# Windowed sink attention in a fused transformer kernel: scores in two fp32r products from stacked high and low halves, one key projection, query projections three tiles ahead

## The chip, the cores and the metric

One core of one Trainium2 chip runs the kernel. The metric is device time in microseconds for one execution, lower is better. Matrix products run on TensorE (PE in the rows), elementwise work on VectorE (DVE) and ScalarE (ACT), some sums on GpSimd (POOL), and SyncE (SP) issues the weight stream. DVE, ACT and PE each take their instructions in the order of their program and meet at semaphores.

## What is computed

Two stacked blocks on 512 tokens of width 1024: an HGRN2 mixer and a convolutional FFN, then shared keys and values with a windowed sink attention and a second FFN, then a latent attention (MLA) and a Hyena mixer. The change touches the windowed attention alone:

```python
k, v = split(rms_norm(h, kv_norm) @ w_kv, 2)             # 2 key/value heads of 64
q = (x @ w_q).reshape(nb, 128, 2, 8, 64)                 # 16 query heads of 64
kb, vb = band(k), band(v)                                # the block before and the own block
scores = einsum('nqkgd,nskd->nkgqs', q, kb) * 64 ** -0.5
scores = where(valid, scores - slopes * dist, -inf)      # 0 <= dist < 128, key_abs >= 0
m = maximum(max(scores), sink)
e = exp(scores - m)
probs = e / (sum(e) + exp(sink - m))
out = einsum('nkgqs,nskd->nqkgd', probs, vb) @ w_o
```

There are four blocks of 128 queries, each with 256 keys. The first block has no block before it, so 128 of its 256 keys are always masked.

## The kernel before

Activations lie transposed: channels on partitions, 512 tokens on the free axis. A weight matrix is streamed in chunks of eight 128x128 tiles. Nearly every product is made in three fp32r passes: the fp32 weights `raw` and the activations are split into a high part (rounded to fp32r, on ACT: `whi`, `khi`) and a low part (the rest, on DVE: `wlo`, `klo`), and `mm_w` adds high x high, high x low and low x high. I call these three matmuls on one 128x128 weight tile a *tile*. A projection (`project`) is eight tiles into one PSUM bank.

The stage `swa` has five parts. (1) Projections: query projection 0 (`wq` 0) and 1, two key projections (`kv` 0 and 1) of eight tiles each, where the weights hold each key head twice, so that it comes out on both halves of the partitions. DVE writes them into `kz`, zeroed ahead by POOL: for key head kv and half x the other half stays zero, and one query tile `qb` with two query heads on its two halves can be used whole. (2) `value_rows`: the values, tokens on partitions, 96 matmuls of 128 columns. (3) Eight *pairs* of query heads, 0 to 7. (4) The output projection `wo`, eight times eight tiles. (5) The residual and the next norm.

A pair i goes through these steps. PE makes the scores, 4 blocks x 2 heads, plain fp32, 128 queries x 256 keys (`softmax`, L685). DVE adds the distance bias into `s` (L2276, eight instructions; the first of them I call the *start* of pair i), takes the maxima (L2281) and makes the negated maximum (L2287). ACT exponentiates in eight instructions with row sums (L1488), then takes the exponential of the sink (L1493). DVE adds, inverts and scales the eight rows (L2299). PE transposes them, four per block (L707, `turn`), ACT copies each block to `pt` (L1503), PE multiplies by the values (L726, fp32), and ACT and DVE split the result into `khi` (L1515) and `klo` (L2307).

The three engines run generators woven by hand. In *round* i they work at `softmax(i + 1)`, `values(i)` and the projection of pair i + 2. On PE a round is: scores of i + 1; then by `SWA_TILES` the eight tiles of projection i + 2, two at a time, with the steps of `values(i)` between them. In rounds 6 and 7, where no projection is left, 6 and 8 tiles of the output projection take their place (`begin`). DVE and ACT use `SWA_AHEAD`: what the projection needs of them comes in the first and middle steps, the exponentials in steps 0 to 3, the sink's exponential in step 4.

## Time and profile before

| | |
|---|---|
| time, median of 3 runs | 2037.94 us (2037.1 to 2038.3) |
| span of the profiled execution | 2037.5 us, 24678 instructions |
| PE / DVE / ACT busy | 97% / 68% / 41% of the span |
| the stage's first query scores, start | 760.64 us |
| start of pair 1, of pair 7 | 778.55, 863.12 us |
| last gap of PE in the stage, end | 887.34 us |

The profile is of one execution, and its own time, first to last instruction, is the span of 2037.5 us; no launch time lies around it in this profile. It is 0.4 us under the median of the runs. A row of the timeline has the start in us from the span's start, the duration, the engine, the line and the operation with its tiles, and in brackets the idle time before it with what ended that. Rows that follow one another overlap a little, since an engine begins an instruction while the end of the one before is still being written; so what an instruction costs in a sequence is the distance from start to start, which I call its pitch. An fp32 matmul of the code is two instructions in the trace (16 rows of scores per pair for 8 in the code).

### The profile page before, as it was taken

The page shows a single profiled execution, that of the slowest core. Times are in us where ns is not written, and L with a number is a line of the kernel's source. Part 1 is how long each engine was busy: PE and PEld are TensorE (multiplying, and loading weights), DVE is VectorE, ACT ScalarE, POOL GpSimd, SP SyncE. Part 2 cuts the span into 40 slices and gives each one's busy share as a digit, 9 for nine tenths or more (in the row PEclk, how much of TensorE's full clock was granted, in tenths as well). Part 3 has the DMA queues.
Part 4 walks back from the last instruction along what each step waited for, and adds up shares of the span by engine and source line. Part 5 has one row for each costly group of instructions (what it writes and reads, how often), then busy time and mean ns, then how long its engine had stood idle before and what let it go on. Part 6 is the DMA issues. An engine that isn't in the chain of part 4 may idle for free.

```text
span 2037.5 us, 24678 instructions
## 1 busy us (share of the span) xinstructions
PE 1978.4 (97%) x9878; PEld 1655.8 (81%) x9878; DVE 1380.5 (68%) x1961; ACT 828.0 (41%) x1259; POOL 233.3 (11%) x234
## 2 busy tenths in 40 slices
PE   8999999999999999999999999999999989999997
PEld 6888887788888888888888888778888878888786
DVE  5577765997789667756764784555555567787774
ACT  5233334442233245544432443444344444454442
POOL 2132231003201230010000001000000101000011
PEclk9999999999999999999999999999999989999998
DMA  5211112345534341114344333311111323232421
GB/s 182 72 56 54 61 53 85 130 150 179 201 138 157 132 137 34 40 64 147 137 159 135 126 133 99 108 62 42 42 32 42 114 73 124 93 126 81 145 94 52
DMA packets 60963, 208.40 MB, mean 102 GB/s; under 512 B 6832, under 2 KB 7152, under 8 KB 59696
## 3 DMA queue, kind: packets, MB, share of 16 engines
q1 hardware_dynamic: 53296, 193.19, 27.9%
q10 hardware_dynamic: 7552, 13.64, 1.9%
q8 instruction: 78, 1.28, 0.2%
q14 instruction: 37, 0.30, 0.0%
HBM read 196.31 MB, written 10.49 MB: 101 GB/s over the span
## 4 chain that ended last, share of the span: by engine, by line
PE 79%; DVE 13%; ACT 5%; issue 2%; POOL 1%; DMA 0%; ACTq 0%; DVEq 0%; SPq 0%
PE PS L324 21%; PE PS L328 20%; PE PS L327 20%; DVE wlo L1879 2%; PE PS L436 2%; PE PS L933 2%; PE PS L331 1%; PE PS L335 1%; PE PS L334 1%; ACT whi L1196 1%; PE PS L922 1%; PE PS L685 1%; PE PS L386 1%; PE PS L726 1%; DVE col_f L2094 1%
## 5 line engine op out<-in xcount | busy, mean ns | idle before, releaser
L324 PE MATMUL PS<-nhi,whi 128*128 128x512 f32 x1456 | 593.1, 407 | 15.4 <-DVE wlo L1879 3.7
L328 PE MATMUL PS<-nhi,wlo 128*128 128x512 f32 x1456 | 571.8, 393 | 0.0
L327 PE MATMUL PS<-nlo,whi 128*128 128x512 f32 x1456 | 570.6, 392 | 0.0
L1879 DVE TENSOR_TENSOR wlo<-raw,whi 128x1024 fp32r<-128x1024 f32 x291 | 368.4, 1276 | 176.5 <-ACT whi L1196 175.4
L1196 ACT ACTIVATE whi<-raw 128x1024 fp32r<-128x1024 f32 x291 | 303.3, 1052 | 209.0 <-PE PS L324 133.2
L324 PEld LDWEIGHTS PS<-nhi,whi 128*128 128x128 f32 x1456 | 276.1, 190 | 78.4 <-issue 11.3
L328 PEld LDWEIGHTS PS<-nhi,wlo 128*128 128x128 f32 x1456 | 275.3, 189 | 59.7
L327 PEld LDWEIGHTS PS<-nlo,whi 128*128 128x128 f32 x1456 | 276.4, 190 | 53.5 <-issue 2.6
L2723 POOL TENSOR_TENSOR diag<-diag,sqb 128x512 f32<-128x512 f32 (+1 forms) x56 | 73.6, 1314 | 780.9 <-ACT sqb L1205 698.3
L324 PE MATMUL PS<-hh_f,whi 128*128 128x512 f32 x352 | 137.8, 392 | 0.0
L327 PE MATMUL PS<-hl_f,whi 128*128 128x512 f32 x352 | 137.7, 391 | 0.0
L328 PE MATMUL PS<-hh_f,wlo 128*128 128x512 f32 x352 | 137.5, 391 | 0.0
L2739 POOL TENSOR_TENSOR sd_f<-ab_f 128x512 f32<-128x512 f32 x32 | 55.3, 1745 | 271.7 <-DVE ab_f L2182 271.1
L2094 DVE SCALAR_TENSOR_TENSOR col_f<-aw_f,scv,col_f 128x1024 f32<-128x1024 f32 x63 | 85.0, 1358 | 0.0
L328 PEld LDWEIGHTS PS<-hh_f,wlo 128*128 128x128 f32 x352 | 66.5, 189 | 14.0
L324 PEld LDWEIGHTS PS<-hh_f,whi 128*128 128x128 f32 x352 | 66.4, 189 | 13.9
L327 PEld LDWEIGHTS PS<-hl_f,whi 128*128 128x128 f32 x352 | 66.5, 189 | 13.7
L1419 ACT ACTIVATE t_f<-gp_f,par 128x512 f32<-128x512 f32 x44 | 35.9, 816 | 94.3 <-DVE gp_f L2199 94.3
L1665 ACT ACTIVATE pt_m<-PS 128x768 f32<-128x768 f32 x32 | 25.9, 811 | 111.8 <-PE PS L922 111.8
L1923 DVE TENSOR_TENSOR hT<-hT,PS 128x512 f32<-128x512 f32 x48 | 32.8, 682 | 52.2 <-PE PS L328 52.1
L436 PEld LDWEIGHTS PS<-qa,kk 128*128 128x128 f32 x448 | 56.0, 191 | 14.2 <-DVE qa L2031 10.3
L1205 ACT ACTIVATE sqb<-hT 128x512 f32<-128x512 f32 x42 | 26.3, 629 | 94.7 <-DVE hT L1923 62.5
(356 smaller groups left out, 3373.2 us busy)
## 6 DMA issues: line engine op xcount, KB each, us to landing
raw<-in_stream SPq DMA_DIRECT2D x291, 512.0 KB, 3.5
aw_f<-in_ada SPq DMA_DIRECT2D x48, 512.0 KB, 4.4
rows<-sd_f ACTq DMA_DIRECT2D x32, 256.0 KB, 2.2
rows_h<-rows SPq DMA_DIRECT2D x8, 1024.0 KB, 6.1
wd_f<-in_decay ACTq DMA_DIRECT2D x16, 256.0 KB, 3.0
hT<-in_xT SPq DMA_DIRECT2D x8, 256.0 KB, 6.9
out<-hT SPq DMA_DIRECT2D x8, 256.0 KB, 2.0
wd_f<-in_filt_out ACTq DMA_DIRECT2D x8, 128.0 KB, 2.9
```

Of the source, the lines that this page charges most:

```text
L324: op = e.matmul(out, hi, xh, start=first, stop=False)
L327: e.matmul(out, hi, xl, start=False, stop=False)
L328: return e.matmul(out, lo, xh, start=False, stop=last)
L436: op = e.matmul(B[b][:, cs], kk[:, z, cs], qx[:, cs], start=True, stop=True)
L933: op = e.matmul(B[6][:, 128 * blk:128 * blk + 128], a.v[:, t, 128 * h:128 * h + 128], a.pt[:, i, 128 * t:128 * t + 128], start=t == 0, sto ...
L1196: e.activation(m.whi[:, c % HL, :], m.raw[:, c % RAW, :], ACT.Copy).then_inc(*s.w_hi.tick(c))
L1419: e.activation(a.t[:, 0, z, :], a.gp[:, z, 2:T + 2], ACT.Identity, bias=pc(cb, f), scale=pc(cw, 44 + f)).then_inc(*s.made_a.tick("c0", lay ...
L1879: e.tensor_tensor(m.wlo[:, c % HL, :], m.raw[:, c % RAW, :], m.whi[:, c % HL, :].bitcast(F), SUB).then_inc(*s.w_lo.tick(c))
L1923: op = e.tensor_tensor(h, h, B[b], ADD)
L2094: e.scalar_tensor_tensor(col[:, v, :], aw[:, n % AW[layer], :], m.scv[:, 2, k, v:v + 1], col[:, v, :], MUL, ADD).then_inc(*s.made_v.tick(" ...
L2723: e.tensor_tensor(acc, acc, m.sqb[:, i % 2 if site != "n4" else 0, 0:width], ADD).then_inc(*s.acc.tick(site, i))
L2739: e.tensor_tensor(a.sd[:, x, :], a.ab[:, 0, :], a.ab[:, 1, :], SUB if x else ADD).then_inc(*s.made_p.tick("sd", n, i, x))
```

## The change

The scores are now two fp32r matmuls. The query tile `qt` is split into `qs`: for half x of the partitions, that head's high part stands on its own half and its low part on the other half (128 rows: 64 high, 64 low). The keys are laid out as `kh`, the high part on both halves, and `kl`, the low part on both halves. `qs` times `kh` plus `qs` times `kl` is the whole product (high and low of the query against the high, then against the low part of the key). `kz` and its zeroing are gone, and the mask tile has one form. One key projection is left instead of two, its high and low parts being copied to both halves by ACT and DVE (four instructions each). Block 0 works on its own 128 keys alone in every step. PE has the second query projection after the key projection, takes value tiles ahead of each block's scores of pair 0, runs the query projections three tiles ahead of the rounds, and has 21 rather than 14 tiles of the output projection before the last values end (one more output is begun).

```diff
+++ after.py
@@ -194,12 +194,14 @@
...
+        a.kh, a.kl = p("kh", [128, 2, T], FR), p("kl", [128, 2, T], FR)
         a.vz = p("vz", [128, 4, 2, 2, 128])
...
+        a.qt = p("qt", [128, 2, T])
+        a.qs = p("qs", [128, 2, 2, T], FR)
         a.s = p("s", [128, 2, 8, 256])
         a.pt = p("pt", [128, 4, 512])
-        a.dist = p("dist", [128, 2, 256])
+        a.kt = a.pt[:, 0, :]
+        a.dist = p("dist", [128, 256])
         a.sm = p("sm", [128, 2, 8, 8])
     with ExitStack() as cs:
         call = m.call = sbt(cs, "call", [128, 2 * KD * TC], FR)
@@ -276,8 +278,12 @@
...
 HG_TILES = [0, 0, 3, 2, 2, 2, 2, 2, 2, 2, 1, 1, 1, 3, 0, 1]
-SWA_TILES = [2, 2, 2, 2, 1, 1, 1, 1, 1]
+SWA_LEAD = 3
+SWA_TILES = [2, 2, 1, 0, 0, 1, 1, 1, 0]
 SWA_AHEAD = [7, 0, 0, 1, 1, 1, 1, 1, 1]
+SWA_BEGUN = [0] * 6 + [1] * 7 + [0] + [2] * 7
+SWA_LAST = {KD - 2: 11, KD - 1: 10}
+head_keys = lambda blk: slice(128, 256) if blk == 0 else slice(0, 256)
...
-        run(project(5, "wq", 1, ("wq", 1), nhi, nlo, lambda: q.wait_ge(*s.h.at("down0", 1, 5)),
-                    then={5: spread("n2")}))
 
         def ready(k):
             q.wait_ge(*s.hid_lo.at("kv", k))
 
-        for n in range(2):
-            run(project(n, "kv", n, ("kv", n), khi, klo, lambda: q.wait_ge(*s.h.at("down0", 1, 6 + n)), ready))
+        run(project(0, "kv", 0, ("kv",), khi, klo, lambda: q.wait_ge(*s.h.at("down0", 1, 6)), ready,
+                    then={5: spread("n2")}))
+        run(project(5, "wq", 1, ("wq", 1), nhi, nlo, lambda: q.wait_ge(*s.h.at("down0", 1, 5))))
...
@@ -675,15 +680,20 @@
             for blk in range(4):
                 if i:
                     q.wait_ge(*s.made_v.at("sc", i - 1, 2 * blk + 1))
-                elif blk < 2:
-                    q.wait_ge(*s.taken_v.at("kz", blk, 1))
+                elif blk == 0:
+                    q.wait_ge(*s.taken_v.at("kv"))
                 else:
-                    q.wait_ge(*s.h.at("down0", 1, blk))
-                q.wait_ge(*s.taken_v.at("wq", i))
-                q.wait_ge(*s.taken_v.at("kz", kv, 1))
+                    q.wait_ge(*s.h.at("down0", 1, 7 if blk == 1 else blk))
+                q.wait_ge(*s.made_a.at("qh", i, 1))
+                q.wait_ge(*s.made_v.at("ql", i, 1))
+                q.wait_ge(*s.made_a.at("kh", kv, 1))
+                q.wait_ge(*s.made_v.at("kl", kv, 1))
+                ks = slice(128 * max(blk - 1, 0), 128 * blk + 128)
                 for x in range(2):
-                    op = e.matmul(B[blk][:, 256 * x:256 * x + 256], a.qb[:, z, 128 * blk:128 * blk + 128],
-                                  a.kz[:, kv, x, 128 * blk:128 * blk + 256], start=True, stop=True)
+                    out = B[blk][:, 256 * x:256 * x + 256][:, head_keys(blk)]
+                    rows = a.qs[:, z, x, 128 * blk:128 * blk + 128]
+                    e.matmul(out, rows, a.kh[:, kv, ks], start=True, stop=False)
+                    op = e.matmul(out, rows, a.kl[:, kv, ks], start=False, stop=True)
                 op.then_inc(*s.sc_mm.tick("s", i, blk))
                 yield
...
-                for j in range(4):
+                for j in range(4) if blk else (1, 3):
...
-        begun = [out(i) for i in range(2)]
-
-        def begin(todo):
-            for i in todo:
+        begun = [out(i) for i in range(3)]
+
+        def begin():
+            for i in SWA_BEGUN:
                 next(begun[i])
                 yield
 
+        pr = chain(value_rows(), *[proj(i) for i in range(2, KD)], begin())
         none = iter(())
         for i in range(-1, KD):
             x = softmax(i + 1) if i + 1 < KD else none
-            if i < 0:
-                pr = value_rows()
-            elif i + 2 < KD:
-                pr = proj(i + 2)
-            else:
-                pr = begin([0] * 6 if i == KD - 2 else [1] * 7 + [0])
             y = values(i) if i >= 0 else none
             for _ in range(5):
+                if i < 0:
+                    next(pr)
                 next(x, None)
-                if i < 0:
-                    next(pr, None)
-            for n in SWA_TILES:
-                for _ in range(n):
-                    next(pr, None)
-                next(y, None)
-                next(x, None)
-            for g in (y, x, pr):
+            if i < 0:
+                for _ in range(KD - 5 + SWA_LEAD):
+                    next(pr)
+            else:
+                for n in SWA_TILES:
+                    for _ in range(n):
+                        next(pr)
+                    next(y, None)
+                    next(x, None)
+            for g in (y, x):
                 run(g)
+        run(pr)
         for i in range(KD):
-            run(begun[i] if i < 2 else out(i))
+            run(begun[i] if i < 3 else out(i))
 
...
             for j in range(8):
-                e.activation(sc[:, j, :], sc[:, j, :], ACT.Exp, bias=sm[:, 2, j:j + 1],
+                row = sc[:, j, head_keys(j // 2)]
+                e.activation(row, row, ACT.Exp, bias=sm[:, 2, j:j + 1],
...
+        def high_q(i):
+            q.wait_ge(*s.taken_v.at("wq", i))
+            if i > 1:
+                q.wait_ge(*s.sc_mm.at("s", i - 2, 3))
+            for x in range(2):
+                ps = slice(64 * x, 64 * x + 64)
+                e.activation(a.qs[ps, i % 2, x, :], a.qt[ps, i % 2, :], ACT.Copy).then_inc(*s.made_a.tick("qh", i, x))
+
+        def proj(i):
+            yield from w.steps(KD)
+            high_q(i)
...
+        for half in range(2):
+            for kv in range(2):
+                q.wait_ge(*s.taken_v.at("kv"))
+                x = kv ^ half
+                e.activation(a.kh[64 * x:64 * x + 64, kv, :], a.kt[64 * kv:64 * kv + 64, :],
+                             ACT.Copy).then_inc(*s.made_a.tick("kh", kv, half))
+        high_q(0)
+        run(w.steps(KD))
+        high_q(1)
...
             elif i + 2 < KD:
-                pr = w.steps(KD)
+                pr = proj(i + 2)
             else:
-                pr = w.steps(6 if i == KD - 2 else KD)
+                pr = w.steps(SWA_LAST[i])
...
-            for n in SWA_AHEAD if i >= 0 else SWA_TILES:
+            for n in SWA_AHEAD:
...
         def take_q(i, b):
             q.wait_ge(*s.filled.at("wq", i))
             q.wait_ge(*s.rb.at("n2"))
-            e.tensor_tensor(a.qb[:, i % 2, :], B[b], m.rb2[:, :], MUL).then_inc(*s.taken_v.tick("wq", i))
+            e.tensor_tensor(a.qt[:, i % 2, :], B[b], m.rb2[:, :], MUL).then_inc(*s.taken_v.tick("wq", i))
+
+        def low_q(i, x):
+            z, ps, po = i % 2, slice(64 * x, 64 * x + 64), slice(64 - 64 * x, 128 - 64 * x)
+            q.wait_ge(*s.made_a.at("qh", i, x))
+            e.tensor_tensor(a.qs[po, z, x, :], a.qt[ps, z, :], a.qs[ps, z, x, :].bitcast(F),
+                            SUB).then_inc(*s.made_v.tick("ql", i, x))
 
         def proj(i):
             yield from w.steps(KD)
             take_q(i, 7)
+            yield
+            low_q(i, 0)
+            yield
+            low_q(i, 1)
...
-                    e.scalar_tensor_tensor(sc[:, 2 * blk + x, :], a.dist[:, min(blk, 1), :], -slope,
-                                           B[blk][:, 256 * x:256 * x + 256], MUL,
+                    at = head_keys(blk)
+                    e.scalar_tensor_tensor(sc[:, 2 * blk + x, at], a.dist[:, at], -slope,
+                                           B[blk][:, 256 * x:256 * x + 256][:, at], MUL,
                                            ADD).then_inc(*s.made_v.tick("sc", i, 2 * blk + x))
                 yield
+            q.wait_ge(*s.made_v.at("sc", i, 1))
+            e.tensor_reduce(sm[:, 0, 0:2], sc[:, 0:2, 128:256], AX_X, ALU.max).then_inc(*s.made_v.tick("mx0", i))
             q.wait_ge(*s.made_v.at("sc", i, 7))
-            e.tensor_reduce(sm[:, 0, :], sc[:, :, :], AX_X, ALU.max).then_inc(*s.made_v.tick("mx", i))
+            e.tensor_reduce(sm[:, 0, 2:8], sc[:, 2:8, :], AX_X, ALU.max).then_inc(*s.made_v.tick("mx", i))
...
-                e.tensor_scalar(sc[:, j, :], sc[:, j, :], sm[:, 7, j:j + 1], None, MUL).then_inc(*s.made_v.tick("pn", i, j))
+                row = sc[:, j, head_keys(j // 2)]
+                e.tensor_scalar(row, row, sm[:, 7, j:j + 1], None, MUL).then_inc(*s.made_v.tick("pn", i, j))
...
-        for n in range(2):
-            run(w.steps(KD))
-            if n == 0:
-                take_q(0, 6)
-                take_q(1, 5)
-            q.wait_ge(*s.filled.at("kv", n))
-            q.wait_ge(*s.made_p.at("kz"))
-            for x in range(2):
-                ps = slice(64 * x, 64 * x + 64)
-                e.tensor_tensor(a.kz[ps, n, x, 128:T + 128], B[n][ps, :], m.rb[ps, :],
-                                MUL).then_inc(*s.taken_v.tick("kz", n, x))
+        q.wait_ge(*s.filled.at("kv"))
+        q.wait_ge(*s.rb.at("n2"))
+        e.tensor_tensor(a.kt, B[0], m.rb[:, :], MUL).then_inc(*s.taken_v.tick("kv"))
+        take_q(0, 6)
+        for half in range(2):
+            for kv in range(2):
+                x = kv ^ half
+                ps = slice(64 * kv, 64 * kv + 64)
+                q.wait_ge(*s.made_a.at("kh", kv, 0))
+                e.tensor_tensor(a.kl[64 * x:64 * x + 64, kv, :], a.kt[ps, :], a.kh[ps, kv, :].bitcast(F),
+                                SUB).then_inc(*s.made_v.tick("kl", kv, half))
+        for x in range(2):
+            low_q(0, x)
+        run(w.steps(KD))
+        take_q(1, 5)
+        for x in range(2):
+            low_q(1, x)
```

How the instructions stand on ACT, round 1, before (`s_s` scores, `sm_s` small columns, `pt_s` transposed probabilities):

```order
L1488 ACTIVATE s_s,sm_s<-s_s,sm_s 128x256 x2
L1503 ACTIVATE pt_s<-PS 128x512
L1488 ACTIVATE s_s,sm_s<-s_s,sm_s 128x256 x4
L1503 ACTIVATE pt_s<-PS 128x512
L1488 ACTIVATE s_s,sm_s<-s_s,sm_s 128x256 x2
L1493 ACTIVATE sm_s<-sm_s 128x8
L1503 ACTIVATE pt_s<-PS 128x512
L1515 ACTIVATE khi_s<-PS 128x512
```

And after the change, the same round:

```order
L1499 ACTIVATE s_s,sm_s<-s_s,sm_s 128x128 x2
L1515 ACTIVATE pt_s<-PS 128x512
L1499 ACTIVATE s_s,sm_s<-s_s,sm_s 128x256 x4
L1515 ACTIVATE pt_s<-PS 128x512
L1499 ACTIVATE s_s,sm_s<-s_s,sm_s 128x256 x2
L1539 ACTIVATE qs_s<-qt_s 64x512 x2
L1504 ACTIVATE sm_s<-sm_s 128x8
L1515 ACTIVATE pt_s<-PS 128x512
L1531 ACTIVATE khi_s<-PS 128x512
```

Two instructions that make the high part of the next query tile stand between the last exponentials and that of the sink (`sm_s<-sm_s`).

On DVE, the same round, before (from the weight split to the next pair's start):

```order
L1879 TENSOR_TENSOR wlo<-raw,whi 128x1024
L2262 TENSOR_TENSOR qb_s<-PS,rb 128x512
L2294 TENSOR_TENSOR sm_s<-sm_s 128x8
L2296 RECIPROCAL sm_s<-sm_s 128x8
L2299 TENSOR_SCALAR s_s<-s_s,sm_s 128x256 x8
L2307 TENSOR_TENSOR klo_s<-PS,khi_s 128x512
L2276 SCALAR_TENSOR_TENSOR s_s<-dist_s,PS 128x256 x8
```

And after the change:

```order
L1914 TENSOR_TENSOR wlo<-raw,whi 128x1024
L2297 TENSOR_TENSOR qt_s<-PS,rb 128x512
L2342 TENSOR_TENSOR sm_s<-sm_s 128x8
L2344 RECIPROCAL sm_s<-sm_s 128x8
L2348 TENSOR_SCALAR s_s<-s_s,sm_s 128x128 x2
L2302 TENSOR_TENSOR qs_s<-qt_s,qs_s 64x512
L2348 TENSOR_SCALAR s_s<-s_s,sm_s 128x256 x2
L2302 TENSOR_TENSOR qs_s<-qt_s,qs_s 64x512
L2348 TENSOR_SCALAR s_s<-s_s,sm_s 128x256 x4
L2356 TENSOR_TENSOR klo_s<-PS,khi_s 128x512
L2322 SCALAR_TENSOR_TENSOR s_s<-dist_s,PS 128x128 x2
L2322 SCALAR_TENSOR_TENSOR s_s<-dist_s,PS 128x256 x6
```

Two instructions that make the low part stand between the eight that scale the rows, ahead of `klo_s`. The maximum is taken in two.

On PE, the step from round 6 to round 7, before (`pt_s,vz_s` are the last values of pair 6, `khi_s` and `klo_s` the operands of the output projection, `ident,s_s` the first transposes of pair 7; the brackets name the semaphores that an instruction still waits for):

```order
L726 MATMUL PS<-pt_s,vz_s 128x128 [waits s_made_a]
L726 MATMUL PS<-pt_s,vz_s 128x128 x3
L324 MATMUL PS<-khi_s,whi 128x512 [waits s_made_v]
L327 MATMUL PS<-klo_s,whi 128x512
L328 MATMUL PS<-khi_s,wlo 128x512
L324 MATMUL PS<-khi_s,whi 128x512
L327 MATMUL PS<-klo_s,whi 128x512
L328 MATMUL PS<-khi_s,wlo 128x512
L707 MATMUL PS<-ident,s_s 128x128 [waits s_made_v]
L707 MATMUL PS<-ident,s_s 128x128
```

And after the change:

```order
L736 MATMUL PS<-pt_s,vz_s 128x128 [waits s_made_a]
L736 MATMUL PS<-pt_s,vz_s 128x128 x3
L330 MATMUL PS<-khi_s,whi 128x512
L333 MATMUL PS<-klo_s,whi 128x512
L334 MATMUL PS<-khi_s,wlo 128x512
L330 MATMUL PS<-khi_s,whi 128x512 [waits s_hid_lo]
L333 MATMUL PS<-klo_s,whi 128x512
L334 MATMUL PS<-khi_s,wlo 128x512
L717 MATMUL PS<-ident,s_s 128x128 [waits s_made_v] x2
L330 MATMUL PS<-khi_s,whi 128x512
L333 MATMUL PS<-klo_s,whi 128x512
L334 MATMUL PS<-khi_s,wlo 128x512
```

The second tile of round 7 now waits for a low part (`s_hid_lo`), that of pair 6; before, the first two tiles of this round needed only low parts made earlier.

## Rows read from the trace of the kernel before

**Rows 1.** The page: busy times; then one window: us, each engine

```profile
PE 1978.4 (97%) x9878; PEld 1655.8 (81%) x9878; DVE 1380.5 (68%) x1961; ACT 828.0 (41%) x1259; POOL 233.3 (11%) x234
...
804.80:819.00 14.20, 14.18 (x87) 12.40 (x86) 10.49 (x27) 7.96 (x23) 0.00 (x0) 1.00 0.11 37
```

**Rows 2.** Timeline of DVE, pairs 1 to 7

```profile
778.55 2.73 DVE L2276 SCALAR_TENSOR_TENSOR s_s<-dist_s,PS 128x256 f32<-128x256 f32 x8
...
792.33 2.76 DVE L2276 SCALAR_TENSOR_TENSOR s_s<-dist_s,PS 128x256 f32<-128x256 f32 x8
...
795.12 2.29 DVE L2281 TENSOR_REDUCE sm_s<-s_s 128x8 f32<-128x2048 f32 x1
...
797.64 0.17 DVE L2287 TENSOR_SCALAR sm_s<-sm_s 128x8 f32<-128x8 f32 x1
...
803.77 2.19 DVE L2299 TENSOR_SCALAR s_s<-s_s,sm_s 128x256 f32<-128x256 f32 x8
...
806.48 2.76 DVE L2276 SCALAR_TENSOR_TENSOR s_s<-dist_s,PS 128x256 f32<-128x256 f32 x8
...
863.12 2.76 DVE L2276 SCALAR_TENSOR_TENSOR s_s<-dist_s,PS 128x256 f32<-128x256 f32 x8
```

**Rows 3.** Timeline of ACT, the exponentials of pairs 1 and 2

```profile
784.05 0.51 ACT L1488 ACTIVATE s_s<-s_s,sm_s 128x256 f32<-128x256 f32 x1 [3.15 <-DVE sm_s L2287]
...
788.95 0.20 ACT L1493 ACTIVATE sm_s<-sm_s 128x8 f32<-128x8 f32 x1
...
803.11 0.20 ACT L1493 ACTIVATE sm_s<-sm_s 128x8 f32<-128x8 f32 x1
```

**Rows 4.** Timeline of PE: scores, value tiles, products of MLA

```profile
790.68 3.62 PE L685 MATMUL PS<-kz_s,qb_s 128*128 128x256 f32 x16
...
761.56 0.28 PE L334 MATMUL PS<-wlo,khi_s 128*128 128x128 f32 x1
...
761.67 0.28 PE L335 MATMUL PS<-whi,klo_s 128*128 128x128 f32 x1
...
1589.95 0.28 PE L907 MATMUL PS<-krh_m,qr_m 128*128 128x256 f32 x1
...
1590.07 0.28 PE L908 MATMUL PS<-krl_m,qr_m 128*128 128x256 f32 x1
```

**Rows 5.** Timelines of DVE and ACT in the MLA stage, splits

```profile
1374.88 0.42 DVE L2453 TENSOR_TENSOR kn_m<-sqb,kn_m 128x256 fp32r<-128x256 f32 x1
...
1375.33 1.40 DVE L2459 TENSOR_TENSOR qr_m<-sqb,qr_m 64x512 fp32r<-64x512 f32 x2
...
1370.63 1.29 ACT L1621 ACTIVATE qr_m<-sqb 64x512 fp32r<-64x512 f32 x2 [4.53 <-DVE sqb L2430]
```

**Rows 6.** Chain of work (first row), then timelines of DVE and PE, head

```profile
742.62 0.79 PE PS L358 x8
...
744.56 5.39 DVE L2315 SCALAR_TENSOR_TENSOR klo_s<-hT,par,khi_s 128x512 fp32r<-128x512 f32 x8
...
750.62 2.36 DVE L1879 TENSOR_TENSOR wlo<-raw,whi 128x1024 fp32r<-128x1024 f32 x2 [0.67 <-ACT whi L1196]
...
749.75 0.39 PE L324 MATMUL PS<-khi_s,whi 128*128 128x512 f32 x1
...
760.64 1.02 PE L685 MATMUL PS<-kz_s,qb_s 128*128 128x256 f32 x4
...
768.31 0.75 DVE L2276 SCALAR_TENSOR_TENSOR s_s<-dist_s,PS 128x256 f32<-128x256 f32 x2 [1.45 <-PE PS L685]
```

**Rows 7.** Timeline of PE at the end of the stage

```profile
874.28 1.16 PE L726 MATMUL PS<-pt_s,vz_s 128*128 128x128 f32 x8 [0.40 <-ACT pt_s L1503]
...
887.34 0.50 PE L324 MATMUL PS<-khi_s,whi 128*128 128x512 f32 x1 [1.41 <-DVE klo_s L2307]
```

**Rows 8.** Windows, PE alone: us, busy, granted clock, DMA share, GB per s

```profile
883.00:890.00 7.00, 5.59 (x38) 1.00 0.02 4
...
1637.00:1644.40 7.40, 4.58 (x10) 0.50 0.00 0
```

32 lines of the change are left out of this document (15 added, 17 removed).

## Prediction

> **What bounds the kernel now.** The page first: PE is busy 97% of the span, DVE 68%, ACT 41% [rows 1]. That is a mean over many stages, so the next view is a window of one pair in the attention stage: of 14.20 us PE is busy 14.18, DVE 10.49, ACT 7.96 [rows 1]. Read alone, this says that PE bounds the stage. The timelines of DVE and ACT say more. Follow one pair from its start to the start of the next, 792.33 to 806.48, 14.15 us [rows 2], through both engines: 2.79 us of bias additions (792.33 to 795.12), 2.72 for the maxima and the small column operations until the first exponential, which begins some 0.20 after L2287's start at 797.64 (it waits for just that, as the releaser in pair 1's row says), 5.27 on ACT until the sink's exponential at 803.11 [rows 3], 0.66 until the scaling begins at 803.77, and 2.71 for the eight scalings and `klo` [rows 2]. The sum is 14.15. DVE begins the next pair without a pause after `klo`. So there is a loop over DVE and ACT which takes the whole period too. DVE's idle quarter isn't spare: it is the time in which it waits for ACT inside the loop. One part of the loop belongs to PE: in pair 1 the ACT stretch is 788.95 - 784.05 = 4.90 us [rows 3], in pair 2 it is 5.27, since there one copy of transposed rows stands between exponentials and waits for PE. Without this hold the loop takes 14.15 - 0.37 = 13.78, which is what the starts of pairs 1 and 2 show, 778.55 to 792.33 [rows 2]. PE's work can therefore shrink by 0.4 us per pair with profit, and after that only the loop counts.
>
> **What PE is spared.** A pair's scores are 16 instructions in the trace, 3.62 us with the tail, a pitch of some 0.216 [rows 4]. The new products are fp32r with 256 columns, for which MLA has the pitch, 1590.07 - 1589.95 = 0.12, and for block 0 with 128 columns, as the value tiles have it, 761.67 - 761.56 = 0.11 [rows 4]. 12 x 0.12 + 4 x 0.11 = 1.88 for 16 x 0.216 = 3.46: 1.6 us less per pair. Two transposes of block 0 fewer are 0.2. That is 1.8 x 8 = 14.4 us. The key projection that is gone is eight tiles; 16 tiles took 749.75 to 760.64 [rows 6], 0.681 each, so 5.4 us. Together 19.8 us of PE. The weight chunk that is no longer streamed costs nothing: the stream is hidden behind PE, whose rows here wait for no chunk.
>
> **What the loop gets.** The order on ACT shows two 64x512 instructions between the last exponentials and the sink's, the order on DVE two 64x512 ones between the scalings. Both stand inside the loop. Nothing hides them: DVE's sum waits for the sink's exponential, which is queued behind the high parts, and the next pair's additions are queued behind the low parts. MLA has the very same split. On ACT two take 1.29 us, on DVE two take 1.40, and the 0.42 us instruction ahead of the first is followed after 0.45, not overlapped [rows 5]. I take 1.3 for the high parts (below 1.29 only if the second's tail is hidden, some 0.1), and 1.55 for the low parts, as each of the two breaks into a row of scalings (bounds 1.2, if they overlapped like full tiles, and 1.6). Block 0 gives back: on DVE 512 columns take 0.69 and 256 take 0.42 [rows 5], 0.135 for 128 columns, so two half additions save 0.27; the maxima have 256 columns of 2048 less, 0.27, but one more instruction, which costs 0.07 to 0.15: 0.2 saved; the two half exponentials about 0.1 each, 0.2; the half scalings between nothing and 0.27 together, I take 0.14. The loop becomes 13.78 - 0.81 + 2.85 = 15.8 us, 1.65 longer than the period now. PE needs about 14.18 - 1.8 = 12.4 us in it and so waits over 3 us per pair; the transposes that ACT's copies wait for are done in time, so the hold is gone.
>
> The query split isn't late elsewhere: the projection, three tiles ahead, ends at the fifth tile of a round, before DVE comes to `qt`. Of the waits for the low part PE's scores are the one that matters; they begin some 1.6 us (four scalings and `klo`) before DVE can begin the pair, and block 0's four matmuls need 0.45. So they are hidden, and so is the wait of each round's first value product for the `klo` of the pair before.
>
> **The head.** Now PE goes from 743.41 (742.62 + 0.79) to 749.75 with eight tiles and the norm's spread, 6.34 us, and through 16 key tiles to 760.64 [rows 6]. Afterwards the key tiles come first, and they need `klo`, whose first is there at 744.56 + 0.69 = 745.25 [rows 5, 6]: PE stands 1.9 us. Then 6.34 and 5.45: query 1 is projected at 757.1. Beside it, DVE's weight split (two from 750.62 in 2.36 us [rows 6], of which one is now due here, to 751.8) comes 1.9 later, 753.7; `kt` and `qt` take 0.6 each; then ACT has six instructions of 0.66 from 754.4 (to 758.4), and DVE six of 0.71 from 755.1, the last following ACT: 759.4. PE fills this with one value tile (twelve matmuls, 1.33). Scores of block 0 start at 759.5, the other blocks 1.33 + 0.49 = 1.82 apart, so the last is there at 759.5 + 5.46 + 0.49 + 0.25 = 765.7. DVE meanwhile does the second query's `qt` and low parts to about 763.6 and has the three first blocks added just by then, so the additions of the last block begin at 765.8 rather than 768.31 [rows 6]. From there to pair 1's start it was 778.55 - 768.31 = 10.24 and is 10.24 - 0.2 - 0.2 - 0.14 = 9.7: 775.5, 3.05 us earlier than now. So the 5.4 us of the key projection are worth about half at this point.
>
> **The middle.** Starts 1 to 7 are six loops: 6 x 15.8 = 94.8, where it was 863.12 - 778.55 = 84.57 [rows 2]. Pair 7 starts at 870.3, 7.2 later than now.
>
> **The tail.** In round 6 nothing is projected, so no split stands in ACT's or DVE's way. From the start of pair 7 to the end of `klo` of pair 6: 2.52 + 2.52 + 4.7 + 0.66 + 2.57, and 0.1 for its end: 13.1, at 883.4. The order on PE shows that the second tile of round 7 waits for this; the first tile is done by then. From the last values of round 6 to the last gap's end it is now 887.34 - 874.28 = 13.06 [rows 7]; without those values (0.91) and the first tile (0.68), without two transposes (0.22), with two more changes between fp32 and fp32r, 0.09 each, 11.4 remain. PE goes on at 894.8. The last gap of 1.41 [rows 7] is filled by two tiles, and 21 rather than 14 of the 64 tiles are done: 43 x 0.681 = 29.3, end 924.1. Now it is 887.34 + 50 x 0.681 = 921.4.
>
> **Sum** against the span: pair 7 starts 7.2 us later (3.05 won at the head, 10.2 lost in six loops); from there to the end of the last gap it is 894.8 - 870.3 = 24.5 for 887.34 - 863.12 = 24.2, 0.3 more (0.6 won by the shorter steps of block 0, the rest the new wait); seven tiles of `wo` done earlier, in PE's waits, give 4.8 back. +2.7 us. The profiled span of 2037.5 becomes 2040.2; the median of the runs lies 0.4 higher, 2040.6. What a measurement of this kernel can tell from no change is about 0.2%, 4.1 us, so 2033.9 to 2042.0.
>
> **Rivals.** (a) *PE is the bound and its saving is the gain.* For it speaks PE's 14.18 of 14.20 us; against it the loop of 13.78 which has no slack. The time: PE's 19.8 less the 1.9 at the head, 17.9 us, 2020. It needs both splits to be hidden. The Trainium skill (Perfetto Trace Analysis, Identifying the Most-Contended Engine) says to find the engine with the highest occupancy and to optimise this one first; by that rule PE is the one to relieve and this rival is what comes. The window's occupancy agrees with it, the loop in DVE's and ACT's rows doesn't. (b) *The splits cost less than in MLA.* If a low part costs 0.6, as `klo` does (2.71 less eight scalings of 0.264 [rows 2]), and a high part 0.55, the loop is 15.25, six of them 3.3 us less and the head 0.6: 2036.7, still no difference that can be told. (c) *Slower: PE's clock.* PE gets waits of over 3 us in each loop. The row of 1637.00 has a granted clock of 0.50, so 1.2 GHz, with PE busy 4.58 of 7.40 us; that of 883.00 stays at 1.00 (2.4 GHz) with 5.59 of 7.00 [rows 8]. Here it is 12.4 of 15.8, nearly the second. At 1.2 GHz a stretch of 3.4 us does 1.7 us less work. In the middle 3.4 us of slack takes this up; it decides only if PE is at the low level for more than some 7 us of every loop, or in the last round: then the round's 10 us become up to 20, +5 or more, 2046. The same page of the Trainium skill (Matmul Optimizations) says that the engine scales power with utilization and matmuls should run back to back, which speaks against this change; the rows say that a busy share of 0.8 still kept the high level. (d) The change does less than it says: no; if the fp32r scores ran at the old pitch, PE would need 14.0 of 15.8 and nothing would change.
>
> **Numbers.** Forecast, a loop of 15.5 to 16.1: 0.60, own range 2037 to 2043; it crosses 2042.0 if the loop is over 16.0, which takes 0.12 of it. (b) 0.17, 2033.5 to 2037.5, of which 0.02 under 2033.9. (a), wholly or half, 0.10. (c) 0.08. Something else that takes over 1 us per loop, slower, 0.05. So faster by over 0.2%: 0.12, slower: 0.25, within: 0.63. The range 2034 to 2044 leaves out (a), most of (c) and the edges.
>
> **What would show it.** Starts of pairs 1 and 7 (L2322) at about 775.5 and 870.3, 15.8 apart; two `qs_s` on ACT of 1.3 us ahead of the sink's exponential, two on DVE; PE busy 12.4 per loop, its wait ahead of the scores named after DVE's low part; a wait of a `wo` tile for `klo_s` early in round 7, and no gap after the last values. I am wrong if pairs start less than 14.5 us apart, or if PE's wait names a copy or a transpose.

## The result, and the profile after

The changed kernel takes 2052.38 us (median of 4 runs, 2049.36 to 2053.21), the kernel before 2037.91 on the same chip (2037.1 to 2038.3): ratio 1.0067, 95% interval 1.0053 to 1.008. It is slower by 14.5 us. 2040.6 with a range of 2034 to 2044 was forecast. The profiled execution took 2051.98 us with a span of 2050.2, close to the median.

The page of the changed kernel, the row that answers to the first of [rows 1]:

```profile
PE 1974.4 (96%) x9838; PEld 1652.6 (81%) x9838; DVE 1385.9 (68%) x1985; ACT 835.3 (41%) x1278; POOL 231.4 (11%) x233
```

PE is busy 4 us less than before although 19.8 us of its work should be gone. Windows over the head of the attention stage say where most of it went. First the changed kernel, PE alone, then the same stretches in the kernel before (us, busy, granted clock, DMA share, GB/s):

```profile
743.00:750.00 7.00, 4.95 (x19) 0.76 0.26 75
750.00:761.00 11.00, 10.75 (x52) 1.00 0.16 48
...
762.90:768.00 5.10, 5.10 (x26) 0.51 0.31 108
768.00:782.00 14.00, 14.00 (x68) 0.50 0.12 37
782.00:786.80 4.80, 4.80 (x15) 0.50 0.00 0
```

```profile
743.00:750.00 7.00, 7.00 (x32) 1.00 0.21 72
...
768.00:782.00 14.00, 14.00 (x99) 1.00 0.13 39
```

Before, PE has the full clock (1.00, 2.4 GHz) all through. Afterwards it has 0.76 in the first stretch, and from 762.9 to 786.8, for 23.9 us, it is at 0.50 (1.2 GHz) and busy every moment of it. A busy PE says nothing here: the same instructions take twice as long. PE's timeline in the changed kernel shows where that begins:

```profile
745.80 0.66 PE L330 MATMUL PS<-khi_s,whi 128*128 128x512 f32 x1 [2.05 <-DVE klo_s L2364]
746.26 0.63 PE L333 MATMUL PS<-klo_s,whi 128*128 128x512 f32 x1
746.68 0.63 PE L334 MATMUL PS<-khi_s,wlo 128*128 128x512 f32 x1
...
761.66 0.30 PE L695 MATMUL PS<-kh_s,qs_s 128*128 128x128 f32 x1 [0.91 <-DVE qs_s L2302]
...
763.26 0.42 PE L337 MATMUL PS<-whi,khi_s 128*128 128x128 f32 x1
763.47 0.41 PE L340 MATMUL PS<-wlo,khi_s 128*128 128x128 f32 x1
...
781.82 0.73 PE L330 MATMUL PS<-nhi,whi 128*128 128x512 f32 x1
...
801.31 0.30 PE L695 MATMUL PS<-kh_s,qs_s 128*128 128x128 f32 x1 [1.49 <-DVE qs_s L2302]
...
803.26 0.40 PE L330 MATMUL PS<-nhi,whi 128*128 128x512 f32 x1
...
935.63 0.39 PE L334 MATMUL PS<-khi_s,wlo 128*128 128x512 f32 x1
```

The first key tile comes 2.05 us late, behind `klo`, as forecast. Its matmuls of 512 columns then follow at 0.42 us (746.26 to 746.68) and not 0.227, for some 3.4 us. The first scores wait 0.91 us for a low part. From 763.0 the matmuls of a value tile, 128 columns, come at 0.21 (763.26 to 763.47) where they took 0.11 [rows 4]. The value tiles last to 781.82; then three projection tiles of 512 columns follow, and about 1 us behind these the full clock is back. The scores of a later pair at full clock run from 801.31 to 803.26. DVE and ACT, the rows that answer to [rows 2, 3, 6]:

```profile
755.86 0.68 DVE L2369 TENSOR_TENSOR pt_s<-PS,rb 128x512 f32<-128x512 f32 x1
...
771.92 0.75 DVE L2322 SCALAR_TENSOR_TENSOR s_s<-dist_s,PS 128x256 f32<-128x256 f32 x2 [2.66 <-PE PS L696]
...
786.75 0.48 DVE L2322 SCALAR_TENSOR_TENSOR s_s<-dist_s,PS 128x128 f32<-128x128 f32 x2 [5.18 <-PE PS L696]
...
834.60 2.46 DVE L2322 SCALAR_TENSOR_TENSOR s_s<-dist_s,PS 128x128 f32<-128x128 f32 x8
...
846.16 0.48 DVE L2348 TENSOR_SCALAR s_s<-s_s,sm_s 128x128 f32<-128x128 f32 x2
846.68 0.69 DVE L2302 TENSOR_TENSOR qs_s<-qt_s,qs_s 64x512 fp32r<-64x512 f32 x1
847.39 0.62 DVE L2348 TENSOR_SCALAR s_s<-s_s,sm_s 128x256 f32<-128x256 f32 x2
...
849.82 0.69 DVE L2356 TENSOR_TENSOR klo_s<-PS,khi_s 128x512 fp32r<-128x512 f32 x1
850.42 2.47 DVE L2322 SCALAR_TENSOR_TENSOR s_s<-dist_s,PS 128x128 f32<-128x128 f32 x8
...
882.07 2.46 DVE L2322 SCALAR_TENSOR_TENSOR s_s<-dist_s,PS 128x128 f32<-128x128 f32 x8
...
894.50 0.69 DVE L2356 TENSOR_TENSOR klo_s<-PS,khi_s 128x512 fp32r<-128x512 f32 x1
```

```profile
844.18 1.27 ACT L1539 ACTIVATE qs_s<-qt_s 64x512 fp32r<-64x512 f32 x2
845.48 0.21 ACT L1504 ACTIVATE sm_s<-sm_s 128x8 f32<-128x8 f32 x1
```

The additions of pair 0's last block come at 771.92, and pair 1 starts at 786.75, after 5.18 us in which DVE waited for nothing but PE's scores. 775.5 was forecast. Pair 7 starts at 882.07 instead of 870.3. From there on the forecast's distances hold again.

### The profile page after: what moved, and what is told of

The parts are those of the page before. It is cut to its first block, busy times and chain, and to the rows that moved or that the text cites. A ratio compares the mean times of both kernels' runs of the same rounds, so it can differ in the third digit from the quotient of the medians.

```text
span 2050.2 us, 24649 instructions
## 1 busy us (share of the span) xinstructions
PE 1974.4 (96%) x9838; PEld 1652.6 (81%) x9838; DVE 1385.9 (68%) x1985; ACT 835.3 (41%) x1278; POOL 231.4 (11%) x233
## 4 chain that ended last, share of the span: by engine, by line
PE 75%; DVE 15%; ACT 6%; issue 3%; POOL 1%; DMA 0%; ACTq 0%; DVEq 0%; SPq 0%
PE PS L330 20%; PE PS L334 19%; PE PS L333 19%; DVE wlo L1914 2%; PE PS L442 2%; PE PS L943 2%; PE PS L337 2%; PE PS L341 2%; PE PS L340 2%; ACT whi L1206 1%; ACT s_s L1499 1%; PE PS L932 1%; PE PS L392 1%; DVE col_f L2129 1%; PE PS L548 1%
## 5 line engine op out<-in xcount | busy, mean ns | idle before, releaser
L442 PE MATMUL PS<-qa,kk 128*128 128x128 f32 x448 | 60.8, 279 | 3.9 <-DVE qa L2066 3.0
```

What stands on the lines that cost most here:

```text
L442: op = e.matmul(B[b][:, cs], kk[:, z, cs], qx[:, cs], start=True, stop=True)
```

## The experiments

Twelve kernels were run. They ran on several chips, but each was compared with the kernel before on its own chip, so two of them are best set against each other by their ratios. The theory of the clock: PE's clock falls at the two waits of the head and stays low through the value tiles, on which pair 1's start hangs. Its rivals: the new order of the head is too long in itself; a wait or a bound in the loops. The theory of the loop: the 15.8 us are the splits' place between ACT and DVE, and PE's saved time becomes time saved as soon as they move to where the loop only waits. The expectations of fill_both, fill_first, fill_second and key_first call the theory of the clock theory 1, and by theory 2 they mean the first rival, the order of work.

### Are the waits of the head the cause?

**fill_both.** Unread matmuls of 512 columns where PE waited, nine ahead of the first key tile and five ahead of the first scores.

```diff
+        def fill(n):
+            c = (len(tiles.spec) - 1) // 8
+            for _ in range(n):
+                e.matmul(B[0], m.whi[:, c % HL, 0:128], nhi[0], start=True, stop=True)
...
-        run(project(0, "kv", 0, ("kv",), khi, klo, lambda: q.wait_ge(*s.h.at("down0", 1, 6)), ready,
+        run(project(0, "kv", 0, ("kv",), khi, klo, lambda: (q.wait_ge(*s.h.at("down0", 1, 6)), fill(9)), ready,
...
                 elif blk == 0:
                     q.wait_ge(*s.taken_v.at("kv"))
+                    fill(5)
```

Expected: 

> The changed kernel with matmuls that nobody reads in PE's two waits at the head of the stage: nine of 512 columns ahead of the first key tile, five ahead of the first scores. They leave out and change nothing of the result. Theory 1 (the slow stretch of PE's clock, 762.9 to 786.8 us, is the loss, and the waits brought it on): the granted clock stays at 1.00 through the head, pair 1 starts at 775 to 776 us instead of 786.75, the loops stay 15.8 us, time 2040 to 2042 us. Theory 2 (the time is lost to the order of work at the head and in the loops, the clock only accompanies it): pair 1 still starts after 784 us and the time stays within 2 us of 2052.

Measured: 2041.27 us (10 runs, 2038.38 to 2043.17), ratio 1.0012 (1.0003 to 1.0022). Its windows, PE alone:

```profile
762.90:768.00 5.10, 5.10 (x48) 1.00 0.03 10
768.00:782.00 14.00, 12.43 (x85) 1.00 0.13 40
```

The clock is 1.00 through the head. The six loops from pair 1 to pair 7 took 95.3 us in the changed kernel and take 95.73 here. Pair 1 starts at 774.74 and pair 7 at 870.47, where 775.5 and 870.3 were forecast. Fourteen matmuls that compute nothing save 11 us (by the two ratios, 0.0055 of 2038), and the forecast's own number, 2040.6, or 1.0013 of the kernel before, comes back. Two small misses cancel in it: pair 1 is 0.8 early, and the loops are 0.9 longer than the 94.8 forecast.

**fill_first** and **fill_second** have one of the two fills each.

Expected: 

> The same with the first wait alone filled (ahead of the first key tile). Theory 1 in the form that the first wait of 2.05 us and its own slow stretch of 3.4 us set the second off: clock 1.00 from 746 to 787 us, time near 2040 to 2042. In the form that the second wait (0.9 us) ahead of the scores does it alone: the stretch from 763 to 787 stays, time 2049 to 2052. Theory 2: no change, 2052.

Expected: 

> The same with the second wait alone filled (ahead of the scores of pair 0). Theory 1, second wait alone the cause: the stretch of 763 to 787 us is gone, the one of 3.4 us at 746 stays, 2042 to 2044. Theory 1, first wait the cause: both stretches stay, 2052. Theory 2: 2052.

Measured: fill_first 2041.59 us as the median of 10 runs, ratio 1.002 (1.0005 to 1.0035), but one of them, the profiled one, took 2054.29, the others 2038.1 to 2042.8. In that one the clock is 0.50 from about 762 on and pair 1 starts at 786.35. fill_second 2045.08 us (8 runs, 2040.93 to 2046.54), ratio 1.0029 (1.0018 to 1.0039); its windows:

```profile
743.00:750.00 7.00, 4.96 (x20) 0.77 0.22 75
...
762.90:768.00 5.10, 5.10 (x47) 1.00 0.30 108
```

So the first wait (2.04 us here) brings the clock down for the key tiles, which costs 2.9 us at pair 1's start (777.65 for 774.74) and 3.8 us in all (2045.08 for 2041.27, on the same chip). By its ratio fill_second lies at 2043.8 on the first chip, within the 2042 to 2044 expected. The wait of 0.91 us ahead of the scores brought the long stretch in one execution of ten when it was the only one, and in the changed kernel, behind the first, in the profiled one and, by the times, in all four. With it filled, none of the 8 executions of fill_second took over 2046.54.

**key_first.** The kernel before with the first key projection put ahead of the second query projection, so that it has the first wait and none of the rest of the change.

```diff
-        run(project(5, "wq", 1, ("wq", 1), nhi, nlo, lambda: q.wait_ge(*s.h.at("down0", 1, 5)),
-                    then={5: spread("n2")}))
...
         for n in range(2):
-            run(project(n, "kv", n, ("kv", n), khi, klo, lambda: q.wait_ge(*s.h.at("down0", 1, 6 + n)), ready))
+            run(project(n, "kv", n, ("kv", n), khi, klo, lambda: q.wait_ge(*s.h.at("down0", 1, 6 + n)), ready,
+                        then={} if n else {5: spread("n2")}))
+            if n == 0:
+                run(project(5, "wq", 1, ("wq", 1), nhi, nlo, lambda: q.wait_ge(*s.h.at("down0", 1, 5))))
```

Expected: 

> The kernel before, with the first key projection ahead of the second query projection and nothing else changed, so that PE waits some 2 us for the low part of the first key operand. Theory 1: a stretch at half clock follows the wait as in the changed kernel, 3.4 us at least (1.7 us of loss) and with the wait 2040 to 2042; if the long stretch comes too, 2048 or more. Theory 2: the wait costs its 2 us, 2039.5 to 2040.

Measured: 2043.55 us (10 runs, 2042.14 to 2044.62), ratio 1.0022 (1.0012 to 1.0031). PE waits 2.04 us, the clock is 0.76 from 743 to 750 and 1.00 from then on; pair 1 starts at 781.68, 3.1 later than in [rows 2]. The first wait alone costs 4.5 us in all (0.0022 of 2038), of which 3.1 stand at pair 1's start. The expectation gave it 2 to 4 us with a fall of the clock and 2 us without one, and the interval leaves out the 2 us. It doesn't bring the long stretch.

### Is it the length of a wait or its place?

**head_order.** The changed kernel with the order of the head turned back (second query projection first), both queries split during the key projection, the keys' splits of key head 0 first, and two value tiles ahead of the scores (the cut leaves out ACT's and DVE's part).

```diff
-        run(project(0, "kv", 0, ("kv",), khi, klo, lambda: q.wait_ge(*s.h.at("down0", 1, 6)), ready,
-                    then={5: spread("n2")}))
-        run(project(5, "wq", 1, ("wq", 1), nhi, nlo, lambda: q.wait_ge(*s.h.at("down0", 1, 5))))
+        run(project(5, "wq", 1, ("wq", 1), nhi, nlo, lambda: q.wait_ge(*s.h.at("down0", 1, 5)),
+                    then={5: spread("n2")}))
+        run(project(0, "kv", 0, ("kv",), khi, klo, lambda: q.wait_ge(*s.h.at("down0", 1, 6)), ready))
...
         pr = chain(value_rows(), *[proj(i) for i in range(2, KD)], begin())
+        next(pr)
...
-                for _ in range(KD - 5 + SWA_LEAD):
+                for _ in range(KD - 6 + SWA_LEAD):
```

Expected: 

> The changed kernel with its head in another order and nothing else: the second query projection ahead of the key projection as before (so that the vector engine's low parts of the key operand are ready when the key projection starts), the query operands of pairs 0 and 1 split during the key projection, the key splits of key head 0 first, and two value tiles instead of one ahead of the first scores. No matmul is added. By the theory that the loss is the tensor engine's clock brought down by the two waits of the head, the granted clock stays at 1.00 from 743 to 785 us, pair 1 starts at about 771 to 775 us (775.5 was forecast for the unchanged order at full clock), the loops stay at 15.8 us, and the median is 2037 to 2041. By the rival that the new order of value tiles and three projections ahead of the first round is itself what is too long at the head, pair 1 still starts after 780 and the median is 2046 or more.

Measured: 2049.32 us (4 runs, 2044.92 to 2050.82), ratio 1.0055 (1.004 to 1.007). That is a miss, and both numbers lie where the rival, the order of the head, had put them. PE's timeline and windows:

```profile
761.42 0.30 PE L695 MATMUL PS<-kh_s,qs_s 128*128 128x128 f32 x1 [2.09 <-DVE kl_s L2382]
```

```profile
762.90:768.00 5.10, 5.10 (x26) 0.50 0.00 0
768.00:782.00 14.00, 14.00 (x62) 0.50 0.10 37
```

PE waits nowhere until the scores, but the keys are now projected last, and the scores wait 2.09 us for their low parts. Behind this one wait the clock is at 0.50 for some 20 us, and pair 1 starts at 783.72. So the windows speak for the clock and not for the rival, which cover (next) settles, and what I said of the clock falls: it doesn't take two waits. One of some 2 us in front of the value tiles was enough.

**cover.** The same order with the splits of the loop moved (dve_split, below), and four value tiles ahead of the first scores. It differs from the kernel `best` (below, two value tiles) only in this.

```diff
         pr = chain(value_rows(), *[proj(i) for i in range(2, KD)], begin())
-        next(pr)
+        for _ in range(3):
+            next(pr)
...
-                for _ in range(KD - 6 + SWA_LEAD):
+                for _ in range(KD - 8 + SWA_LEAD):
```

Expected: 

> The new order of the head and the splits of pairs 2 to 7 on the vector engine, with four value tiles instead of two ahead of the first scores (each 1.33 us at full clock), so that the 2.09 us in which the tensor engine waited for the low parts of the keys are covered by work of the kernel's own. No matmul is added. By the theory that this wait alone brought the clock down there: clock 1.00 from 741 to 787 us, pair 1 starts at 770 to 774 instead of 783.5, loops of 13.05 us, median 2020 to 2024. If the clock stays low without a wait, the value tiles themselves are the cause, pair 1 starts after 780 and the median is 2032 or more.

Measured: 2026.22 us (4 runs, 2022.68 to 2027.35), ratio 0.9941 (0.9926 to 0.9955). `best` has 2034.56 (0.998), so the two value tiles gave 8 us; 2020 to 2024 was expected, 2 us lower. A window of cover:

```profile
760.00:773.00 13.00, 11.37 (x84) 1.00 0.12 40
```

Scores start without a wait and the clock is 1.00 until the head's value tiles are done. Then a later wait of 2.54 us brings it down too; PE's timeline there:

```profile
773.91 0.44 PE L717 MATMUL PS<-ident,s_s 128*128 128x128 f32 x2 [2.54 <-ACT vz_s L1487]
```

```profile
774.60:778.00 3.40, 3.40 (x11) 0.50 0.00 0
```

Pair 1 starts at 774.28, not 770 to 774, but 9.25 us ahead of `best`: the order of the head isn't what is too long. The fall behind the later wait lasts 3.4 us, while PE works mostly on projection tiles of 512 columns.

### Why does the low clock last so long?

**fill_mid.** The changed kernel with 12 unread matmuls of 512 columns behind the second value tile, so behind both waits.

```diff
+                if k == 2:
+                    rb_read("n2")()
+                    for _ in range(12):
+                        e.matmul(B[7], w[0], nhi[0], start=True, stop=True)
                 for t in range(4):
```

Expected: 

> The changed kernel with 12 matmuls of 512 columns, read by nobody, put between the second and the third value tile, that is behind both waits of the head. By the theory that the low clock lasts for 24 us because the value tiles have 128 columns a matmul, and that 512 columns a matmul bring it back: the low stretch that begins near 762 ends within the 12 matmuls or soon behind them (12 at the pitch of 0.43 us are 5.1 us), so before 773, and the rest of the value tiles run at a pitch near 0.11; pair 1 starts at about 781 to 784, 3 to 6 us earlier than in the changed kernel, although 3 to 5 us of matmuls are added; the median is 2046 to 2050. By the rival that the clock's return does not hang on the form of the matmuls, it comes back near 785 as before, pair 1 starts 5 us later (near 792), and the median is 2055 or more.

Measured: 2049.11 us (4 runs, 2046.41 to 2050.09), ratio 1.0056 (1.0039 to 1.0073). PE's timeline:

```profile
764.23 3.40 PE L669 MATMUL PS<-nhi,whi 128*128 128x512 f32 x12
...
767.63 0.27 PE L341 MATMUL PS<-whi,klo_s 128*128 128x128 f32 x1
767.74 0.27 PE L337 MATMUL PS<-whi,khi_s 128*128 128x128 f32 x1
```

```profile
761.80:765.20 3.40, 3.40 (x16) 0.50 0.51 159
765.20:768.00 2.80, 2.80 (x17) 1.00 0.01 3
```

Ahead of them the value tiles run at 0.21, behind them at 0.11 (767.63 to 767.74). The full clock is back at 765.2, 1 us after the first of the twelve, where the changed kernel had 0.50 until 786.8. Pair 1 starts at 780.85 instead of 786.75, although 3.4 us of matmuls were added. None of the four executions came near the 2055 of the rival; the gain in the median (1.0056 for 1.0067) is within the two intervals, so what speaks is the profile and that the added matmuls cost nothing. The long stretches of the other kernels say the same: in the changed kernel and in head_order the clock came back only among the 512-column projection tiles (from 781.82 and 779.83) or just behind them, at 786.9 and 782.3. So the form of what PE runs decides how long it stays slow. Which part of the form counts, the width of a matmul or something that goes with it, no run separates.

### Does such a wait always lower the clock?

The traces hold a case that nobody planned. In the MLA stage every kernel has the same wait of 2.63 us ahead of the same projection. In the kernel before and in fill_second, each with the window behind it:

```profile
1323.79 0.47 PE L324 MATMUL PS<-nhi,whi 128*128 128x512 f32 x1 [2.63 <-DVE call L2377]
```

```profile
1323.79:1330.00 6.21, 6.21 (x31) 1.00 0.24 79
```

```profile
1329.11 0.47 PE L330 MATMUL PS<-nhi,whi 128*128 128x512 f32 x1 [2.63 <-DVE call L2438]
```

```profile
1329.11:1334.11 5.00, 5.00 (x15) 0.66 0.08 15
```

Of the 14 profiled executions, the clock was lowered at this wait in 7 and stayed at 1.00 in 7. The nine single waits of 2.04 to 2.94 us in the head all had a fall beside them. So a wait of 2 us makes a fall likely and not certain.

### The theory of the loop

**dve_split.** fill_both, and the high parts of pairs 2 to 7 made by DVE straight behind `qt` in the slot in which it waits for the exponentials. The low parts go there too.

```diff
         def proj(i):
             yield from w.steps(KD)
-            high_q(i)
...
             take_q(i, 7)
-            yield
-            low_q(i, 0)
-            yield
-            low_q(i, 1)
+            q.wait_ge(*s.taken_v.at("wq", i))
+            q.wait_ge(*s.sc_mm.at("s", i - 2, 3))
+            for x in range(2):
+                ps = slice(64 * x, 64 * x + 64)
+                e.tensor_scalar(a.qs[ps, i % 2, x, :], a.qt[ps, i % 2, :], 1.0, None,
+                                MUL).then_inc(*s.made_v.tick("qh", i, x))
+            for x in range(2):
+                low_q(i, x)
```

Expected: 

> The version with both waits of the head filled (2041.3 us), and the high parts of the query operands of pairs 2 to 7 made by the vector engine behind the taking of the queries, in the time in which it waits for the exponentials (4.33 us idle there), the low parts with them. It takes 1.27 us from the scalar engine ahead of the sink's exponential and 1.38 us from the vector engine behind it, in 6 of 7 loops. If the splits on the loop between vector and scalar engine are what made it 15.8 us and TensorE has nothing to do with it, the loop becomes 13.1 to 13.2 us (TensorE's work in it, some 12.5, comes close), and the median falls by 15 to 16 us to 2025 to 2027. If TensorE or the weight stream is the bound behind it, the loop stays above 14.5 and the median above 2033.

Measured: 2023.06 us (4 runs, 2022.03 to 2025.36), ratio 0.9931 (0.9916 to 0.9946), 1.9 us below what was expected. DVE's timeline of one pair, and a window of it (all engines in the order of [rows 1]):

```profile
811.92 2.46 DVE L2331 SCALAR_TENSOR_TENSOR s_s<-dist_s,PS 128x128 f32<-128x128 f32 x8
...
818.75 0.88 DVE L2317 TENSOR_SCALAR qs_s<-qt_s 64x512 fp32r<-64x512 f32 x2
819.65 1.40 DVE L2307 TENSOR_TENSOR qs_s<-qt_s,qs_s 64x512 fp32r<-64x512 f32 x2
821.73 0.17 DVE L2351 TENSOR_TENSOR sm_s<-sm_s 128x8 f32<-128x8 f32 x1 [0.68 <-ACT sm_s L1510]
```

```profile
811.92:824.96 13.04, 12.36 (x85) 10.95 (x84) 11.94 (x31) 7.30 (x24) 0.00 (x0) 1.00 0.13 40
```

The loop is 824.96 - 811.92 = 13.04 us. DVE is busier in it than ever (11.94), since four more instructions fill its wait, of which 0.68 remains. PE is busy 12.36 of 13.04, so most of its saving has become time. From pair 1 to pair 7 it is 78.25 us (772.78 to 851.03), where fill_both has 95.73: 17.5 us. Six loops of 15.8 would give 16.6 of this; the rest are two loops of fill_both that took 16.2 us.

**es_first.** fill_both, with the high parts still on ACT, but behind the sink's exponential (one `yield` more ahead of `high_q(i)`).

Expected: 

> The version with both waits of the head filled (2041.3 us), the high parts of the query still on the scalar engine but behind the sink's exponential instead of ahead of it. This takes 1.27 us out of the loop in 6 of 7 loops, while the vector engine keeps its 1.38 us of low parts: loops of 14.5 to 14.6 us instead of 15.8, median 2033 to 2035. If the transposed block that comes behind it on the scalar engine (or the low part of the output, which waits for the last value matmuls) is late next, the loop falls by less than 0.7 us and the median stays above 2037.

Measured: 2032.42 us (10 runs, 2027.7 to 2036.62), ratio 0.9973 (0.9963 to 0.9983), just under the 2033 to 2035 expected. Loops of 14.51 us, as expected. The two high parts changed places with one short instruction, and 1.3 us per pair are gone.

**split_only.** The changed kernel with dve_split's edit and no fill.

Expected: 

> The changed kernel, its head as it is, with only the splits of pairs 2 to 7 moved to the vector engine (nothing filled). The two losses should add: loops of 13.05 us take 6 x 2.7, some 16 us, from 2052.4, and the head keeps its 10 to 11 us of low clock in most executions: median 2034 to 2037; in executions where the clock does not fall, 2023 to 2026. By the rival that the low clock and the loop are one effect (the waits of the loop being what keeps the clock low), the shorter loop removes it and the median is below 2028.

Measured: 2034.86 us (10 runs, 2032.22 to 2038.45), ratio 0.9984 (0.9974 to 0.9993). Loops of 13.05 us, pair 1 at 786.09, a clock of 0.50 from 768 to 782. The two losses add (0.9984 is 10.8 us above dve_split's 0.9931), and the shorter loop doesn't cure the clock.

**best.** head_order with dve_split's edit.

Expected: 

> The new order of the head (no added matmuls) and the splits of pairs 2 to 7 on the vector engine together. If both theories hold, the clock is 1.00 through the head, pair 1 starts at 771 to 775, the loops are 13.1 us, and the median is 2020 to 2026, below the kernel before by 12 us or more. If one of them is wrong, it is above 2033.

Measured: 2034.56 us (10 runs, 2029.8 to 2037.21), ratio 0.998 (0.997 to 0.9989). Loops of 13.05, but the wait of head_order is there too (2.09 us), and pair 1 starts at 783.53. The median lies 8.6 us above the range expected, for the same reason as in head_order; cover mends it.

### One part of the change alone

**one_key.** The kernel before with one key projection for both key heads, scores still in fp32.

```diff
-        for n in range(2):
-            run(project(n, "kv", n, ("kv", n), khi, klo, lambda: q.wait_ge(*s.h.at("down0", 1, 6 + n)), ready))
+        run(project(0, "kv", 0, ("kv",), khi, klo, lambda: q.wait_ge(*s.h.at("down0", 1, 6)), ready))
...
-                e.tensor_tensor(a.kz[ps, n, x, 128:T + 128], B[n][ps, :], m.rb[ps, :],
+                own = slice(64 * n, 64 * n + 64)
+                e.tensor_tensor(a.kz[ps, n, x, 128:T + 128], B[0][own, :], m.rb[own, :],
```

Expected: 

> The kernel before with one part of the change alone: one key projection for both key heads instead of two with each head doubled (24 matmuls of 512 columns less, 5.5 us of the tensor engine), the scores still in fp32. In the head nothing covers the tensor engine's work, so the gain should be most of 5.5 us less what the four writings of the key operand (0.69 us each on the vector engine) now take together ahead of the first scores: median 2033 to 2036. If the tensor engine's saved time in the head is lost to the waits for the key operand, and its clock falls there, the median is 2040 or more.

Measured: 2039.38 us (10 runs, 2036.82 to 2044.35), ratio 1.0009 (0.9999 to 1.0019), no difference that can be told. 2033 to 2036 was expected. PE's timeline:

```profile
758.62 1.22 PE L684 MATMUL PS<-kz_s,qb_s 128*128 128x256 f32 x4 [2.94 <-DVE kz_s L2326]
...
762.10 2.02 PE L684 MATMUL PS<-kz_s,qb_s 128*128 128x256 f32 x4
...
769.89 0.27 PE L331 MATMUL PS<-whi,khi_s 128*128 128x128 f32 x1
770.00 0.28 PE L334 MATMUL PS<-wlo,khi_s 128*128 128x128 f32 x1
```

5.5 us of PE's work are gone, a wait of 2.94 comes, and the clock is low from 759.5 to 769.8; pair 1 starts at 781.58, 3 us later than in [rows 2]. The gain of this part went into the wait and the clock, as the second half of the expectation had it. Here the low stretch ends among value tiles, after 10 us; between them stand fp32 scores (2.02 us a block) where head_order has the short fp32r ones.

## Why the prediction was wrong

The step that failed is rival (c), PE's clock, in the part **The rivals**: "In the middle 3.4 us of slack takes this up; it decides only if PE is at the low level for more than some 7 us of every loop, or in the last round". It was priced for the loops and the last round and not for the head, which has no slack: value tiles, three projection tiles and pair 1's scores stand in one line there. The part **The head** worked out a wait of 1.9 us and ran everything behind it at full clock. The runs put 11 us in its place: 2052.38 against 2041.27 with the waits filled. Its chance of 0.08 leant on one row, a busy share of 0.8 at the full clock [rows 8], which is a mean and doesn't tell short gaps from one wait of 2 us; the wait in that row was of 1.41 us [rows 7].

By the other steps:

- *The loop*: 15.8 forecast; 850.42 - 834.60 = 15.82 measured. High parts 1.27 for two (1.3 taken), low parts 0.71 and 0.72 between the scalings (the first 846.68 to 847.39), 1.43 for 1.55. Six loops took 95.3 us for 94.8. The waits of a loop came as single ones of at most 1.5 us, and two of the six waits of 1.49 us ahead of scores had a fall of 3.4 us beside them. In fill_both the clock is 0.93 from 795 to 870; four of its six loops are 15.8 all the same and two 16.2, so the slack takes nearly all of it up, as said.
- *PE's price*: the scores 803.26 - 801.31 = 1.95 us for the 1.88 forecast. PE is busy 12.86 per loop for 12.4, probably with tails that nothing overlaps where it waits.
- *The head*: the first wait 2.05 for 1.9. `kt` starts at 755.86 for 753.7: the key tiles at half clock, the norm's spread and the weight split behind it later. First scores 761.66 for 759.5, last block's additions 771.92 for 765.8, pair 1 786.75 for 775.5. At full clock, in fill_both, it is 774.74.
- *The tail*: `klo` of pair 6 ends at 895.19, 13.1 after pair 7's start, as forecast; the end of `wo` is 935.63 + 0.23 = 935.86, 53.8 after it, as forecast (924.1 - 870.3).
- *The sum*: pair 1 11.25 late, the loops 0.5; the stages behind `wo` took 1.7 us less than before (1114.3 for 1116.0). Their granted clock was 0.99 in this execution and 0.98 in that of the kernel before, which may be why; it isn't shown. Span 2050.2 for 2040.2.
- *Rival (a)*, PE as the bound, 2020, did not come, but its condition, that both splits be hidden, was right: dve_split meets it, with the head's waits filled, and has 2023.06. The Trainium skill (Perfetto Trace Analysis, Identifying the Most-Contended Engine) says to optimise the engine with the highest occupancy first. The runs differ from it here: none gained by PE's saving until DVE's and ACT's loop was shortened, and shortening this loop, with PE's work the same, gave 17 us.
- For *rival (c)* the Trainium skill (Perfetto Trace Analysis, Matmul Optimizations) says that the matmul engine scales its power with utilization and that matmuls should run back to back. The runs agree: 14 unread matmuls in the waits gave 11 us.

What stays open: why the fall behind a wait of 0.91 us came in one execution of ten in fill_first. Why the clock falls at one and the same wait in some executions and not in others, as at the 2.63 us in MLA, isn't told by these runs either. In the changed kernel filling the first wait removed the long stretch in 9 executions of 10, filling the second in all 8, so neither wait brought it alone as a rule.
